# Hymba decoder layer on one core: VectorE's order in a recurrent turn drawn up anew, two squares and the W1T copy on ScalarE, first masks, copies and flips by half

## What is computed

```python
kk = (k * k_k).reshape(B, S, H, N)
kk = kk / jnp.maximum(jnp.sqrt(jnp.sum(kk * kk, axis=-1, keepdims=True)), 1e-12)
k = k * (1.0 + (a - 1.0) * k_a)
def step(state, inp):
    r_t, w_t, k_t, v_t, kk_t, a_t = inp
    sa = jnp.einsum('bhvk,bhk->bhv', state, -kk_t)
    state = state * w_t[:, :, None, :] + sa[..., None] * (kk_t * a_t)[:, :, None, :] + v_t[..., None] * k_t[:, :, None, :]
    return state, jnp.einsum('bhvk,bhk->bhv', state, r_t)
o = (o - mu) * lax.rsqrt(var + GN_EPS) * ln_x_w + ln_x_b
bonus = jnp.sum(r_h * k_h * r_k, axis=-1, keepdims=True) * v_h
o = (o + bonus) * g
```

## Time and profile before

| | |
|---|---|
| median of 3 runs | 2067.25 us (2066.12 to 2069.53) |
| profiled execution | 2067.76 us, span 2066.0 us |
| TensorE busy | 2026.0 us (98%) |
| VectorE busy | 1155.8 us (56%) |
| ScalarE busy | 861.7 us (42%) |
| GpSimd busy | 142.6 us (7%) |
| chain that ended last, by engine | PE 92%, DVE 5%, issue 1% |
| mean granted TensorE clock | 0.994 of full |

### The profile page before, as it was taken

How to read it: one execution, slowest core, us unless ns; L and a number is a source line. 1 busy time by engine, 2 the same in 40 slices (tenths; PEclk the granted TensorE clock), 3 DMA queues, 4 the chain that set the end, 5 groups by cost and what they waited for, 6 DMA issues and landing times.

```text
span 2066.0 us, 27601 instructions
## 1 busy us (share of the span) xinstructions
PE 2026.0 (98%) x11416; PEld 1691.7 (82%) x11416; DVE 1155.8 (56%) x1023; ACT 861.7 (42%) x833; POOL 142.6 (7%) x113
## 2 busy tenths in 40 slices
PE   8999999999999999999897999999999999999999
PEld 6888888888888889888776888888888888888887
DVE  4455545555455565766788545455554555545564
ACT  6333333343343355854333345433333433333353
POOL 0000000000000000344323100000000000000000
PEclk9999999999999999999999999999999999999999
DMA  7565555555555547666312455656555655556554
GB/s 260 185 200 185 186 196 186 193 188 188 192 193 186 189 150 221 205 195 209 99 41 69 148 190 183 196 184 195 191 184 192 192 188 188 193 187 199 184 184 143
DMA packets 190049, 373.62 MB, mean 181 GB/s; under 512 B 7110, under 2 KB 16962, under 8 KB 189980
## 3 DMA queue, kind: packets, MB, share of 16 engines
q1 hardware_dynamic: 186300, 361.47, 54.2%
q0 software_dynamic: 3680, 11.15, 1.9%
HBM read 363.94 MB, written 5.52 MB: 179 GB/s over the span
## 4 chain that ended last, share of the span: by engine, by line
PE 92%; DVE 5%; issue 1%; POOL 0%; DMA 0%; ACT 0%; SPq 0%; DVEq 0%; POOLq 0%
PE PS L363 29%; PE PS L364 29%; PE PS L365 29%; PE PS L420 1%; PE PS L384 1%; DVE X L1653 0%; DVE XT L1666 0%; PE PS L1334 0%; DMA x_resid<-in_x 0%; DVE kk L1577 0%; DVE wlo L349 0%; PE PS L1298 0%; DVE AB L1639 0%; DVE AK L1639 0%; DVE k L1593 0%
## 5 line engine op out<-in xcount | busy, mean ns | idle before, releaser
L349 DVE TENSOR_TENSOR wlo<-raw,whi 128x2048 fp32r<-128x2048 f32 (+1 forms) x338 | 777.5, 2300 | 762.5 <-PE PS L365 757.3
L340 ACT ACTIVATE whi<-raw 128x2048 fp32r<-128x2048 f32 (+1 forms) x338 | 643.2, 1904 | 988.7 <-PE PS L365 980.4
L363 PE MATMUL PS<-whi,xT_hi 128*128 128x512 f32 (+2 forms) x1936 | 752.5, 389 | 0.0
L365 PE MATMUL PS<-whi,xT_lo 128*128 128x512 f32 (+2 forms) x1936 | 747.9, 386 | 0.0
L364 PE MATMUL PS<-wlo,xT_hi 128*128 128x512 f32 (+2 forms) x1936 | 747.5, 386 | 0.0
L365 PEld LDWEIGHTS PS<-whi,xT_lo 128*128 128x128 f32 x1936 | 363.5, 188 | 73.4
L363 PEld LDWEIGHTS PS<-whi,xT_hi 128*128 128x128 f32 x1936 | 363.6, 188 | 72.2 <-issue 0.4
L364 PEld LDWEIGHTS PS<-wlo,xT_hi 128*128 128x128 f32 x1936 | 363.7, 188 | 71.6
L363 PE MATMUL PS<-whi,hT_hi 128*128 128x512 f32 x680 | 264.8, 389 | 0.1
L365 PE MATMUL PS<-whi,hT_lo 128*128 128x512 f32 x680 | 264.6, 389 | 0.0
L364 PE MATMUL PS<-wlo,hT_hi 128*128 128x512 f32 x680 | 264.5, 389 | 0.0
(11 more groups left out here) (330 smaller groups left out, 1112.1 us busy)
## 6 DMA issues: line engine op xcount, KB each, us to landing
raw<-in_w_gate SPq DMA_DIRECT2D x88, 1024.0 KB, 5.2
raw<-in_w_up SPq DMA_DIRECT2D x88, 1024.0 KB, 5.2
raw<-in_w_down SPq DMA_DIRECT2D x88, 1024.0 KB, 5.1
raw<-in_w_in SPq DMA_DIRECT2D x28, 1024.0 KB, 5.5
raw<-in_w_out SPq DMA_DIRECT2D x16, 1024.0 KB, 5.2
raw<-in_w_ple_gate SPq DMA_DIRECT2D x16, 1024.0 KB, 5.1
raw<-in_w_q_b SPq DMA_DIRECT2D x3, 1024.0 KB, 5.3
z_scratch<-zst POOLq DMA_DIRECT2D x6, 512.0 KB, 3.2
```

Of the source, the lines that this page charges most:

```text
L340: nc.scalar.activation(whi[:, n % WHI, 0:wd], raw[:, n % RAW, 0:wd], ACT.Copy).then_inc(hi_ready, 1)
L349: nc.vector.tensor_tensor(wlo[:, n % WLO, 0:wd], raw[:, n % RAW, 0:wd], f32(whi[:, n % WHI, 0:wd]), ALU.subtract).then_inc(lo_ready, 1)
L363: nc.tensor.matmul(acc, a, whi[:, n % WHI, c], start=st, stop=False)
L365: ins = nc.tensor.matmul(acc, b, whi[:, n % WHI, c], start=False, stop=en)
```

## The change

- Masks, the first copy into X and the first flip go by half: 4 systems, then the other 4. AK is masked after both.
- Per turn two squares (kk, and the centred outputs) go to ScalarE, into `tmp`, and so does the W1T copy. Group 0 and the last group's outputs keep theirs on VectorE.
- `out_centre` stands before level 0, `out_spread` and the bonus behind level 0; the share tmn behind level 2, the key's sum and k behind level 3; the read product, its gain and its sum in and behind `state`; xT_lo first in `state`.
- TensorE's transposes of og stand ahead of X*Y, and go through bank 1 in place of bank 3.
- GpSimd makes the next bonus and the key's power after the three og products; for the last group VectorE makes these three products.
- In the last turn the two W_out splits stand one place later.

The core of the diff (the counts of semaphores, which only follow the halves, are left out):

```diff
                 power(hsg[:, 1, :], "minus_half", out_pow)
-                if r < GROUPS - 2:
-                    key_norm(pool, r + 2)
+                if r == GROUPS - 1:
+                    return
                 pool.wait_ge(out_pow, r + 1)
...
             key_norm(pool, 1)
+            gate_ahead(0)
             for r in range(GROUPS):
-                gate_ahead(r)
                 finish(r)
+                if r < GROUPS - 1:
+                    gate_ahead(r + 1)
+                if r < GROUPS - 2:
+                    key_norm(pool, r + 2)
...
                     ins.then_inc(ws_done, 1)
+                if c == 1 and r:
+                    pe.wait_ge(heads_out, 2 + r)
                 if c == 2:
...
                     own_tokens(pe, 0)
-                if c == 0 and r:
-                    pe_out(pe, r - 1)
                 if nxt is not None and c == 1:
-                    if r:
-                        pe.wait_ge(heads_out, 2 + r)
                     turn(pe, nxt, 0)
...
+            pe.wait_ge(ak_ready, 2 * min(r + 2, GROUPS))
...
-                    ins = nc.tensor.transpose(PS[:, 3, (2 * pr + t) * P:(2 * pr + t + 1) * P], og[:, t, pr * P:(pr + 1) * P], ident)
+                    ins = nc.tensor.transpose(PS[:, 1, (2 * pr + t) * P:(2 * pr + t + 1) * P], og[:, t, pr * P:(pr + 1) * P], ident)
...
+                if it:
+                    pe_out(pe, it - 1)
...
                                          ACT.Copy).then_inc(inv_qs, 1)
+                if n == 3 and 0 < r < GROUPS - 1:
+                    act_square_key(act, r + 1)
                 for part in ahead(r, n):
                     act_gates(act, r + 1, part)
+                if n == 3 and r == 0:
+                    act_square_key(act, 1)
+                if n == 0 and r:
+                    act_square_out(act, r - 1)
                 if n == len(INV) - 2:
                     act_y(act, r)
-                if r == GROUPS - 1 and n in LATER[:2]:
+                if r == GROUPS - 1 and n == 2:
                     act.wait_ge(front_ready, 4 * GROUPS)
-                    split_hi(act, WOUT + n - LATER[0])
+                    split_hi(act, WOUT)
+                if r == GROUPS - 1 and n == 4:
+                    act.wait_ge(bonus_ready, GROUPS)
+                    split_hi(act, WOUT + 1)
...
                 nc.scalar.activation(U[:, t, :], PS[:, 6 + t, 0:256], ACT.Copy, scale=-1.0).then_inc(w2_ready, 1)
+            if r:
+                act_out(act, r - 1)
+            act.wait_ge(w1_done, r + 1)
+            nc.scalar.activation(W1T[:, :, :, :].rearrange("p a t (c n) -> p c (a t) n", c=2),
+                                 PS[:, 4:6, 0:256].rearrange("p c (x n) -> p c x n", x=4), ACT.Copy).then_inc(w1_ready, 1)
             for c in range(1, NCHUNK):
...
                     dve.wait_ge(*loaded(r))
-                    tt(kk[:, :, :], k_, bc_t(gc[:, 0, :]), ALU.mult)
-                    tt(tmn[:, :, :], kk[:, :, :], kk[:, :, :], ALU.mult)
-                    v.reduce_sum(hsf[:, 0, :], by_head(tmn[:, :, :]), axis=X_AXIS).then_inc(kk_var, 1)
-                elif step == "own key":
-                    dve.wait_ge(kk_var, r + 1)
+                    v.tensor_tensor(kk[:, :, :], k_, bc_t(gc[:, 0, :]), ALU.mult).then_inc(kk_scaled, 1)
+                elif step == "key sum":
+
+                    if r == 0:
+                        dve.wait_ge(kk_scaled, 1)
+                        tt(tmn[:, :, :], kk[:, :, :], kk[:, :, :], ALU.mult)
+                    else:
+                        dve.wait_ge(kk_squared, r)
+                    v.reduce_sum(hsf[:, 0, :], by_head(tmp[:, :, :] if r else tmn[:, :, :]), axis=X_AXIS).then_inc(kk_var, 1)
+                elif step == "key share":
+                    if r == 0:
+                        dve.wait_ge(kk_var, 1)
                     dve.wait_ge(gates_ready, 2 * r + 2)
                     chain(v.scalar_tensor_tensor(tmn[:, :, :], aa[:, :, :], -1.0, bc_t(gc[:, 1, :]), ALU.add, ALU.mult))
+                elif step == "own key":
                     chain(v.scalar_tensor_tensor(k2[:, :, :], tmn[:, :, :], 2.0, k_, ALU.add, ALU.mult))
...
-                def masked(dst, mask, done, ready, b0):
-                    dve.wait_ge(done, r + 1)
-                    for par in range(2):
-                        v.tensor_tensor(dst[:, :, :].rearrange("p (x par) c -> p x par c", par=2)[:, :, par, :],
-                                        PS[:, b0 + par, :].rearrange("p (x c) -> p x c", x=4),
-                                        const(mask).unsqueeze(1).broadcast_to([P, 4, P]), ALU.mult).then_inc(ready, 1)
-                masked(AB, "mask_b", ab_done, ab_ready, 4)
-                dve.wait_ge(xinit, r + 1)
-                dve.wait_ge(ab_ready, 2 * r + 2)
-                v.memset(gate_step[:, 2:3], 0.0)
-                v.copy_predicated(odd_cols(X[:, :, :], 1), joins(1, 0, 8), odd_cols(AB[:, :, 0:CHUNK], 1)).then_inc(up_ready, 1)
-                dve.wait_ge(up_ready, 11 * r + 1)
-                flip(XT, X, 0, 8).then_inc(low_ready, 1)
-                masked(AK, "mask_k", ak_done, ak_ready, 0)
+                def masked(dst, mask, ready, b0, h):
+                    v.tensor_tensor(dst[:, 4 * h:4 * h + 4, :].rearrange("p (pr par) c -> p par pr c", par=2),
+                                    PS[:, b0:b0 + 2, 256 * h:256 * h + 256].rearrange("p par (pr c) -> p par pr c", pr=2),
+                                    const(mask).unsqueeze(1).unsqueeze(1).broadcast_to([P, 2, 2, P]), ALU.mult).then_inc(ready, 1)
+                dve.wait_ge(ab_done, r + 1)
+                for h in range(2):
+                    mine = slice(4 * h, 4 * h + 4)
+                    masked(AB, "mask_b", ab_ready, 4, h)
+                    dve.wait_ge(xinit, r + 1)
+                    dve.wait_ge(ab_ready, 2 * r + h + 1)
+                    v.memset(gate_step[:, 2:3], 0.0)
+                    v.copy_predicated(odd_cols(X[:, mine, :], 1), joins(1, 0, 4), odd_cols(AB[:, mine, 0:CHUNK], 1)).then_inc(up_ready, 1)
+                    dve.wait_ge(up_ready, 12 * r + h + 1)
+                    flip(XT, X, 4 * h, 4 * h + 4).then_inc(low_ready, 1)
+                dve.wait_ge(ak_done, r + 1)
+                for h in range(2):
+                    masked(AK, "mask_k", ak_ready, 0, h)
...
-                            dve.wait_ge(low_ready, 9 * r + 2 * n + h + 2)
+                            dve.wait_ge(low_ready, 10 * r + 2 * n + h + 3)
...
-                            for step in {2: ("key",), 3: ("own key", "read"), 4: ("unit key", "learned")}[n]:
+                            for step in {2: ("key", "key share"), 3: ("key sum", "own key"), 4: ("unit key", "learned")}[n]:
...
-                        elif n in LATER[:2] and h == 1:
+                        elif n in LATER[1:] and h == 1:
...
-                            split_lo(dve, WOUT + n - LATER[0])
+                            split_lo(dve, WOUT + n - LATER[1])
...
-                            out_centre(before)
-                        if before is not None and (n, h) == (1, 1):
...
+                            front(r, "bonus")
...
-                dve.wait_ge(w1_done, r + 1)
-                v.tensor_copy(W1T[:, :, :, :].rearrange("p a t (c n) -> p c (a t) n", c=2),
-                              PS[:, 4:6, 0:256].rearrange("p c (x n) -> p c x n", x=4)).then_inc(w1_ready, 1)
-                if nxt is not None:
-                    front(nxt, "read gain")
+                if r:
+                    out_lo(r - 1)
...
                             ins.then_inc(s_ready, 1)
-                    if c == 1 and r:
-                        out_lo(r - 1)
-                    if nxt is not None and c == 0:
-                        front(nxt, "read sum")
                     if nxt is not None:
...
                             dve.wait_ge(exps_ready, 5 * nxt + 5)
+                        if c == 1:
+                            front(nxt, "read")
                         for k in ((0,), (1,), (2, 3), ())[c]:
                             with_decay(nxt, k)
+                        if c == 3:
+                            front(nxt, "read gain")
...
-                dve.wait_ge(out_centred, r + 1)
-                tt(tmp[:, :, :], oo[:, :, :], oo[:, :, :], ALU.mult)
+                if r == GROUPS - 1:
+                    dve.wait_ge(out_centred, r + 1)
+                    tt(tmp[:, :, :], oo[:, :, :], oo[:, :, :], ALU.mult)
+                else:
+                    dve.wait_ge(out_squared, r + 1)
                 chain(v.reduce_sum(hsg[:, 1, :], by_head(tmp[:, :, :]), axis=X_AXIS))
...
+            def out_last(r):
+
+                dve.wait_ge(norm_used, r + 1)
+                dve.wait_ge(out_pow, r + 1)
+                tt(by_head(og[:, :, :]), by_head(og[:, :, :]), per_head(hsg[:, 1, :]), ALU.mult)
+                tt(og[:, :, :], og[:, :, :], bonus[:, r % 2, :, :], ALU.add)
+                dve.wait_ge(exps_ready, 5 * r + 5)
```

(8 more changed lines are left out.)

19 lines of the change are left out of this document (13 added, 6 removed).

## The result

| | before | changed |
|---|---|---|
| median of 4 runs each | 2067.94 us | 2053.09 us |
| range | 2066.12 to 2069.53 | 2051.16 to 2055.61 |
| ratio to before, 95% interval | | 0.9929 (0.9912 to 0.9946) |
| the profiled execution, its span | 2067.76, 2066.0 | 2055.61, 2053.8 |

The change makes the kernel 14.85 us faster, 0.7%; the forecast was 2055.1 and 11.8 to 12.2 us less. In the two profiled executions the difference is 12.15 us, which is the sum of the prediction to the digit. That is chance: the terms are not those of the sum, as the windows of the four turns show. They are cut as the earlier trace rows were, from the first mask of a group to the next (columns: us, then PE, PEld, DVE, ACT, POOL busy, PEclk, DMA share, GB/s).

The account below looks back on a forecast made before the run. It took VectorE's chain of waits in the four recurrent turns as the bound. Turn gains of 2.1, 3.1, 3.15 and 3.8 us sum to 12.15, taking the profiled 2067.76 to 2055.6, so a median of 2055.1; range 2051 to 2062.5.

Parts of the forecast that it names:

- step 1: Opening of a turn: masks, first copy and flip by halves cost VectorE 0.28 us more per turn.
- step 2: Before level 0: centring (1.58 us) fills VectorE's 1.76 us wait; level 0 only 0.1 us later, level 1 at TensorE's pace.
- step 4: Last level: less VectorE work behind level 3, so last copies start 19.6 us into the turn, 1.9 us earlier.
- og ready at A+14.4 (forecast 14.5): Sign to look for: og ready about 14.5 us after a turn's first mask, its variance coming behind level 0.
- the rival "GpSimd's result ends last": TensorE waits for GpSimd's og before X*Y; whole gain only 6.2 us, 2061.1 us; chance 0.10.
- step 6: X*Y to first state product: TensorE's chain through U and xT_hi ends last; state at 23.5 us, 3.0 us earlier.
- the end wait: End of kernel: TensorE's 0.64 us wait for GpSimd's last og goes, with three products on VectorE.
- Step 3: Before level 3: three ops become two; 0.3 us added for GpSimd's bonus meeting the key product; level 3 at 16.65 us.
- Step 5: Before the unit key: GpSimd's power of the key takes 1.63 us and comes later; VectorE waits 0.45 us.
- Step 7: First state product to next turn's first mask: net -0.2 us; turn 1's extra 1.7 us of low clock kept.
- The rival with the high clock: TensorE's clock stays high, returning 1.7 us in turn 1 and some 0.7 elsewhere: 2052.7 us; chance 0.12.
- Turn 3: Last turn: 3.8 us less, from 2.3 before the first state, 0.85 before U and 0.64 at the end.

Follow-up runs that it names:

- e1: Changed kernel with masks, first copy and flip again over all eight systems instead of by halves; 2052.80 us, ratio to before 0.9935.
- e7: Changed kernel with the centring of the outputs back behind level 0 and its sum of squares behind level 1; 2054.19 us, ratio to before 0.9929.
- e8: Changed kernel with the last group's three finishing products back on GpSimd instead of VectorE; 2053.78 us, ratio to before 0.9929.
- e5: Changed kernel, turns 1 and 2: key product a level earlier, its ScalarE square behind level 2's Q copies, read product behind level 3; 2051.51 us.
- e12: Changed kernel with the outputs' path back as before: key's power ahead of GpSimd's three products, og transposes behind the state chain's first chunk; 2060.30 us.
- e2: Changed kernel with the W1T copy moved from ScalarE back to VectorE, in front of xT_lo; 2055.35 us, ratio to before 0.9950.
- e10: Kernel before with 48 extra 64x64 TensorE products in front of X*Y in turns 1 to 3; 2068.39 us, ratio to before 1.0002.
- e6: Changed kernel with the read product back behind level 3 in turns 0 to 2; 2050.89 us, ratio to before 0.9916.
- e9: Changed kernel with e5's and e6's moves together, plus the first state product placed ahead of xT_lo; 2049.62 us, ratio to before 0.9916.
- e11: Kernel before without two GpSimd products per group's output, the variance factor and the added bonus; 2061.34 us, ratio to before 0.9977.
- e3: Changed kernel with both squares moved from ScalarE back to VectorE; 2056.43 us, ratio to before 0.9955.
- e4: Changed kernel, turns 1 and 2: key product a level earlier, its ScalarE square ahead of level 2's Q copies, read before unit key; 2056.63 us.

## Why the prediction was right, and where it was not

**What held.** The total, by errors that cancel; that nothing outside the turns moves; step 1 (+0.28 a turn: e1 gives 0.27 and 0.10, and 0.42 up to level 3 of turn 3); step 2, and that the levels run at TensorE's pace (level 0 at A+5.92 against 5.84, level 2 at 13.04 against 13.0; e7); step 4 (last copies at A+19.64 against 19.6, k at 0.68; behind a level 3 that came 0.3 us late, it took 2.69 and not 2.95 us); og ready at A+14.4 (forecast 14.5), so the rival "GpSimd's result ends last" fell; step 6's size, S at A+23.64 against 23.5; the end wait (0.79 in e8 against 0.64). In step 1 the prediction took from the Trainium skill, "VectorE: DVE Perf Modes", section on the TRN2 errata, a fixed cost of 58 cycles, 0.12 us for two instructions. The same section says that 58 under-predicts and gives a measured fixed term of about 150 cycles, by which, an estimate, it is 0.31 us; e1's 0.27 agrees with that. Two slips of the sum itself: steps 6 and 7 add up to -3.2, where -3.1 and -3.15 were used, and the low end of the range works out at 2051.6, not 2051.

**Step 3** allowed 0.3 us for the key product's meeting with GpSimd; it took 1.70 instead of 0.65, and level 3 came at A+16.95 instead of 16.65. With the key product elsewhere (e5) it came at A+16.69. In turn 0 I had seen no GpSimd work at that place at all. There the key product took 1.45 and the share 2.85 us beside GpSimd's mixing of the projections, so level 3 gained 0.07 and not 0.65 us. The last copies there wait 1.80 us for TensorE and gain 0.11; S gains 1.12 us, nearly all of it behind them.

The traces give the price of such a meeting. The key product begins at 1043.82, 0.11 us behind the start of GpSimd's bonus product; that ends at 1044.98, and the key product 0.54 us later. It is the same wherever it happens: between 985 and 1160 us of the 14 traces 72 VectorE products of 128x512 with two SBUF inputs are stretched to over 0.75 us, and each ends 0.54 to 0.56 us behind the end of a GpSimd product. The 29 stretched 8-column operations end 0.02 to 0.04 us behind one (e12: 1049.09 + 1.00 against 1049.03 + 1.04). So the step waits out the GpSimd product that has begun before it, by 0.05 us at the least in the 72; one key product, in turn 0 of e1, kept its 0.65 us with the same lead of 0.05. Where VectorE begins first it keeps its time, and GpSimd's product is the longer one: a square of 0.69 us at 1128.15 in the changed kernel, and GpSimd's product from 1128.25 takes 1.74 us instead of 1.27. The Trainium skill's rule in "SBUF — State Buffer", section "Who interferes with whom", fits the rows of two inputs, and the copies and flips of one input next to them, which keep 0.29 and 0.45. The 8-column operation has one input and is held all the same; the section leaves room for it, since it exempts one-input operations only outside the 2-port perf modes, but no trace shows in which mode it ran.

**Step 5** put the power at 1.63 us, from one row; it takes 1.96, and VectorE waits 0.93 and not 0.45. Its place is not the reason: e12 has it back in the old place, and it takes 2.01. The key's power took 1.63 to 1.67 in the three kernels built on before and 1.96 to 2.04 in the eleven others; why is open.

**Step 6, "this chain, not VectorE's, ends last", is wrong.** The chain that sets S is key sum, GpSimd's power, unit key, b, xT_lo. e2 shows it (0.6 us more on VectorE is 0.4 to 0.9 us in S), and e5 shows the other chain 0.47 us ahead, where S comes once VectorE's is out of the way. The 0.33 us that the power takes more than its row of before is most of that distance. The two chains are nearly equal, and I had named the wrong one.

**Step 7, "I keep those 1.7 us", is the mis-sized term.** S to A fell by 2.19 us where I had -0.2. In the table's marks it was 12.46 us before, 10.78 in e10's turn 1 with the same order at clock 1.00, and 10.28 after: 1.68 us are clock and 0.50 order. Turn 2, where the clock of before was low ahead of S only, gives the same 0.50 for the order (10.79 to 10.29). I had taken turn 0's 10.91 us as the price without a slow stretch, and it has one (0.65 in the window shown under e10). At clock 1.00 the order of before takes 10.01 us there and the new one 10.30, so in turn 0 the order cost 0.29 us and the -0.53 seen is clock. e6 names the cost: with the read product out of the S chain S to A is 10.01 or 10.02 in turns 0 to 2. The prediction had put it into a wait, free of charge; it costs 0.27 or 0.28 us a turn. The rival with the high clock, at 0.12, is what happened.

Over many executions: the kernel before was granted 0.991 to 0.998 and took 2072 to 2062 us with it (23 executions beside e9 to e11: five at 0.991 took 2069.69 to 2073.09, three at 0.997 took 2062.75 to 2064.29). The changed kernel had 0.997 to 1.000. At 0.997, then, 10.5 of the 14.85 us remain (2063.7 less the 2053.24 of the changed kernel's one execution at 0.997) and some 4 go with the clock; along the slope of those 23 executions, 1.27 us for a thousandth, before would take 2061.9 at the 0.999 of the changed kernel's profiled execution, and 6 would. Both are estimates from executions that differ in more than the clock: e3's five spread from 0.995 to 0.999 and took 2056.23 to 2056.71 us, so a low mean need not cost time.

**Turn 3** should have given 3.8 us and gave 1.79 in the profiled execution, because a slow stretch of 1.6 us fell into the dense W_out products, with 0.79 us of idle time ahead of it. Without these it gives 43.69 - 39.05 = 4.6 us (e8). Before, two slow stretches lay in this turn as well, one in the inverse (0.57 over 1112 to 1116) and one around X*Y and the first S (0.65 and 0.93 over 1128 to 1136); what they cost is not shown. So two errors cancelled, 1.9 us too much gained in turn 1, 1.7 of it clock, and 2.0 us too little in turn 3, clock and idle time, and with them the profiled sum comes out at -12.15.

**What the parts are worth, by undoing them:** the outputs' path with GpSimd's order 7.2 us (e12), the squares 3.3 (e3), W1T 2.3 (e2), the centring's place 1.1 (e7), the end 0.7 (e8), masks by tile nothing (e1), read out of the last level -2.2 (e6). Each is a difference of medians of different groups of runs and uncertain by a us or two, and the turns bear out their order; e12's 7.2 holds TensorE's wait for og and its clock besides VectorE's steps.

**Open.** What makes the clock fall. In these traces a fall followed waits of TensorE of 1.30 (e4), 2.57 (e12), 1.54 (e10) and 2.30 us (before), and none followed the 0.66 of e5 or the 1.15 of the changed kernel in turn 1. But the same wait comes with a fall and without one: 1.47 us before the first product with S in turns 1 and 2 of e3, with a fall behind the first alone; 1.23 us in turn 0 of before (fall) and of e10 (none); 2.24 us in the opening of turn 0 of e10 (0.57 over 996 to 1000) and of before (1.00). And e10 shows that filling one wait moves the fall. Not settled either is the idle time of 0.2 to 1.2 us with no releaser, in turn 3 of the changed kernel, e1, e2, e4, e5, e7 and e12, and once, 1.03 us, in turn 1 of e10.

## What to carry to other kernels

Where two engines share work at the end of a serial chain, ask first in which microseconds a GpSimd product overlaps a step of VectorE that something waits for, and move it under steps that something else bounds: without it S comes 2.04 and 1.88 us later in turns 1 and 2 (e12). Price a meeting by its start: the step that begins second waits for the other engine's product to end. When an operation moves to another engine with a wait, list what stands behind it in that queue; one square put ahead of two copies cost 2.77 us in one turn before level 3, and some 5 us in all (e4 against e5). And when the forecast adds one duration to each of two chains that end 0.4 us apart, keep both: the next gain lies in whichever is last by then.

## What the runs showed of the hardware

- A VectorE product of 128x512 with two SBUF inputs that meets a GpSimd product begun before it ends 0.54 to 0.56 us behind that product's end, in all 72 stretched cases of these traces; an 8-column operation of one input ends 0.02 to 0.04 us behind it, in all 29. The latter takes 0.17 us alone, and 0.42, 0.70 or 1.00 us there.
- A low clock of TensorE costs by where it falls: 1.6 us in dense 128x512 products, 1.57 us over the S chain of before's turn 1, 0.81 us in its turn 0, 0.51 us in e3's turn 1.
- The kernel before spreads over 10 us from execution to execution (2062.4 to 2073.1 beside e1 to e11), along its granted clock; e9, with waits of TensorE of at most 0.70 us in turns 1 and 2, spreads over 1.3 us at 0.999 in all five, but e5, with the same longest wait there, over 2.3 us at 0.998 to 1.000.
- GpSimd's power of 128x8 took 1.63 to 1.67 us or 1.96 to 2.04 us, with operands of the same shape, and in e12 2.01 in the very place in which it took 1.63 before.
